# The causal mask of the attention scores: added by TensorE inside the score's bank, where VectorE added it before

## What is computed

```python
s = jnp.einsum('bhmqd,bhmkd->bhmqk', qi, k).astype(jnp.float32) * scale
s = jnp.where(kpos[None, :] <= qpos[:, None], s, -jnp.inf)
p = jax.nn.softmax(s, axis=-1)
...
return jnp.einsum('bhqk,bhkd->bhqd', pd.astype(v.dtype), v)
```

## Time and profile before

| what | before |
|---|---|
| median of three runs | 916.38 us |
| lowest and highest | 915.25 and 921.18 us |
| the profiled execution, its own time | 915.04 us |
| span of its instructions | 913.3 us |
| granted TensorE clock, mean | 0.992 |

### The profile page before, as it was taken

The page is one execution under the profiler, slowest core; times in us unless marked ns, Lnnn a source line. Parts: engine busy times, 40 slices in busy tenths (PEclk is TensorE's granted clock), DMA queues, the critical chain, the costliest instruction groups (busy, mean ns, idle before and its releaser), DMA issues.

```text
span 913.3 us, 16032 instructions
## 1 busy us (share of the span) xinstructions
PE 875.5 (96%) x6422; PEld 820.9 (90%) x6422; DVE 611.5 (67%) x1155; ACT 410.9 (45%) x727; POOL 111.4 (12%) x123
## 2 busy tenths in 40 slices
PE   6999999899999999989999999999999999999996
PEld 6998998898888777888999999999998999999994
DVE  4784687662979789745686478945665776676672
ACT  6456666231011254735344875444344444453451
POOL 0149666100011000400000000100000000000000
PEclk9999999999999899999999999999999999999998
DMA  9454433281452400344665243654453455645741
GB/s 368 169 183 126 123 104 111 79 334 49 140 174 103 184 1 1 93 152 142 215 217 168 94 135 110 220 184 175 149 188 134 141 181 187 229 142 182 231 139 47
DMA packets 37786, 139.41 MB, mean 153 GB/s; under 512 B 4304, under 2 KB 4432, under 8 KB 37456
## 3 DMA queue, kind: packets, MB, share of 16 engines
q1 hardware_dynamic: 37424, 136.90, 43.8%
q10 hardware_dynamic: 288, 1.48, 0.5%
HBM read 137.32 MB, written 1.05 MB: 152 GB/s over the span
## 4 chain that ended last, share of the span: by engine, by line
PE 88%; DVE 7%; issue 2%; ACT 2%; DMA 1%; POOL 0%; DVEq 0%; SPq 0%; ACTq 0%; POOLq 0%
PE psum L578 21%; PE psum L579 21%; PE psum L580 21%; PE psum L577 15%; PE psum L731 3%; PE psum L713 2%; PE psum L652 1%; PE psum L724 1%; DVE h_rows L1748 1%; PE psum L856 1%; DVE w_lo L1594 1%; DVE h_lo L1560 1%; DMA rows<-in_mem 1%; PE psum L641 1%; ACT act_tmp L1219 0%
## 5 line engine op out<-in xcount | busy, mean ns | idle before, releaser
L1594 DVE TENSOR_TENSOR w_lo<-raw,w_hi 128x1024 fp32r<-128x1024 f32 x180 | 212.2, 1222 | 86.2 <-ACT w_hi L1151 85.1
L1151 ACT ACTIVATE w_hi<-raw 128x1024 fp32r<-128x1024 f32 x204 | 206.0, 1052 | 41.3 <-PE psum L580 30.3
L578 PE MATMUL psum<-h_hi,w_hi 128*128 128x256 f32 x704 | 199.5, 283 | 0.6 <-issue 0.6
L579 PE MATMUL psum<-h_lo,w_hi 128*128 128x256 f32 x704 | 199.2, 283 | 0.0
L580 PE MATMUL psum<-h_hi,w_lo 128*128 128x256 f32 x704 | 199.2, 283 | 0.0
L578 PE MATMUL psum<-w_hi,h_hi 128*128 128x256 f32 x576 | 166.6, 289 | 4.1 <-DVE h_lo L1560 4.1
L580 PE MATMUL psum<-w_hi,h_lo 128*128 128x256 f32 x576 | 163.7, 284 | 0.0
L579 PE MATMUL psum<-w_lo,h_hi 128*128 128x256 f32 x576 | 163.6, 284 | 0.0
L578 PEld LDWEIGHTS psum<-h_hi,w_hi 128*128 128x128 f32 x704 | 135.1, 192 | 1.6 <-issue 1.4
L579 PEld LDWEIGHTS psum<-h_lo,w_hi 128*128 128x128 f32 x704 | 135.1, 192 | 0.2
L580 PEld LDWEIGHTS psum<-h_hi,w_lo 128*128 128x128 f32 x704 | 135.1, 192 | 0.0
(11 more groups left out here) (276 smaller groups left out, 1138.5 us busy)
## 6 DMA issues: line engine op xcount, KB each, us to landing
raw<-in_blocks SPq DMA_DIRECT2D x208, 512.0 KB, 4.4
first<-in_blocks SPq DMA_DIRECT2D x40, 512.0 KB, 4.8
w_late<-in_blocks SPq DMA_DIRECT2D x4, 512.0 KB, 7.6
early<-in_early SPq DMA_DIRECT2D x1, 1579.0 KB, 16.3
attention<-in_late ACTq DMA_DIRECT2D x1, 1376.0 KB, 6.9
rows<-in_mem SPq DMA_DIRECT2D x2, 512.0 KB, 4.3
x<-in_x SPq DMA_DIRECT2D x1, 1024.0 KB, 8.4
out_x<-h_rows SPq DMA_DIRECT2D x2, 512.0 KB, 2.6
```

The lines of the kernel that those rows point to most:

```text
L578: nc.tensor.matmul(out, lhs[0], rhs[0], start=start, stop=False, skip_group_check=shared_bank)
L579: nc.tensor.matmul(out, lhs[0], rhs[1], start=False, stop=False, skip_group_check=shared_bank)
L1151: nc.scalar.activation(split_part(w_hi, q), raw[:, q % RAW_SLOTS, :], ACT.Copy).then_inc(w_hi_ready, 1)
L1594: V.tensor_tensor(split_part(w_lo, q), raw[:, q % RAW_SLOTS, :], split_part(w_hi, q).bitcast(F32), ALU.subtract).then_inc(w_lo_vector, 1)
```

## The change

The triangle is added by TensorE. After the score product of a causal unit for a half t, a second product accumulates onto the diagonal block of that half: the identity times the triangle, both as fp32r tiles of 128 x 128. VectorE's addition is dropped. ScalarE makes the two fp32r tiles once, ahead of its copy of the memory keys, and TensorE waits for them once, ahead of the first layer's units.

```diff
+        mask_parts = sb("mask_parts", [P, 2, P], F32R)
...
                         mm = nc.tensor.matmul(psum[:, SCORE_BANK + score.slot(i + j), u.seg(t)],
-                                              q[:, t * P:(t + 1) * P], k[:, 0:u.keys[t]], start=True, stop=True)
+                                              q[:, t * P:(t + 1) * P], k[:, 0:u.keys[t]], start=True, stop=True,
+                                              skip_group_check=u.causal)
+                        if u.causal:
+                            at = u.seg(t).start + t * P
+                            mm = nc.tensor.matmul(psum[:, SCORE_BANK + score.slot(i + j), at:at + P], mask_parts[:, 0, :],
+                                                  mask_parts[:, 1, :], start=False, stop=True, skip_group_check=True)
...
+            pe.wait_ge(mask_ready, 1)
             chunk_read(pe, "b_v")
...
             act.wait_ge(lam_neg_exp, 1)
+            act.wait_ge(loaded["early"], 16)
+            link(nc.scalar.activation(mask_parts[:, 0, :], ident, ACT.Copy))
+            nc.scalar.activation(mask_parts[:, 1, :], E("causal")[:, 0:P], ACT.Copy).then_inc(mask_ready, 1)
+            act.wait_ge(mask_ready, 1)
             source("mk0", mk_t[:, 0], 1.0)
...
                     link(V.tensor_tensor(bank[:, 0:u.width], bank[:, 0:u.width], E("cmp_mask"), ALU.add))
-                elif u.causal:
-                    corners = [v.rearrange("p (b k) -> p b k", k=P)[:, 0:3:2, :] for v in (bank[:, 0:3 * P], E("causal"))]
-                    link(V.tensor_tensor(corners[0], corners[0], corners[1], ALU.add))
```

More of the change, by code:

```diff
@@ L442, in build @@
         ws_ready = sem("ws_ready")
+        mask_ready = sem("mask_ready")
         rest_done = sem("rest_done")
```

## The result

The changed kernel takes 972.36 us (median of four runs, 964.80 to 978.07) against 918.72 us for the kernel before beside it (four runs, 915.25 to 921.18): a ratio of 1.058 [1.050, 1.067]. It is slower, as forecast, by 53.6 us and not by 32, and lies above the range. The four executions of the changed kernel differ among themselves as their clock does: spans of 963.0, 969.0, 972.2 and 976.3 us go with mean granted clocks of 0.972, 0.963, 0.962 and 0.957. Its profiled execution is the shortest of them, 964.80 us with a span of 963.0; against the profiled execution of before that is 49.7 us of span.

What follows compares the result with a forecast made beforehand. TensorE, busy for 96% of the span, was taken as the bound. 915.04 us profiled plus 34.9 for mask products less 2.7 of waits is 947.2, and 1.34 more for the median gives 948.5 us; range 934 to 959.

Steps and rivals of the forecast that it cites:

- The pair: TensorE, last transpose to next load in a causal pair: 3.24 us instead of 1.06, 34.9 us more in 16 pairs.
- the sum: Whole kernel: 915.04 us profiled plus 34.9 less 2.7 is 947.2; as a median 948.5 us.
- changes of height: TensorE in a causal pair: each switch between tile heights leaves about 0.10 us empty; six more cost 1.24 us.
- the units' company: TensorE in a causal pair: the two units' scores no longer share the array, costing 0.65 us.
- The waits in the second layer: TensorE's four waits ahead of the second layer's transposes end: 2.7 us off, least nothing, about 3 at most.
- VectorE's later scores: A pair's scores reach VectorE up to 2 us later, covered by projection products: costed at nothing.
- ScalarE's two copies: Two 128 x 128 copies ahead of the memory keys' copy: 0.8 us, absorbed by ScalarE's idle time.
- The narrow fp32r stream: Rival: mask products stream as slowly as plain fp32, 0.216 us instead of 0.06; 958 us in all; chance 0.13.
- The loads: Rival: six more weight loads in a pair hide behind streams, 10.3 us less, 938 us in all; chance 0.12.
- merely take its place: Rival: mask products only join TensorE's row, 0.11 us each, pairs still side by side; 921 us; chance 0.06.
- VectorE does not bind: Denies the rival that VectorE binds and its relief makes the kernel 2 us faster, 914 us; chance 0.03.
- The clock falls: Rival: more drained, idle unit time lowers TensorE's clock; ten microseconds at 1.2 GHz add 5 us; 954 and more; chance 0.04.

Runs made afterwards that it cites:

- e1_grouped: Changed kernel with all scores of a causal pair first, then its four mask products: 923.10 us, ratio 1.005.
- e4_by_half: Changed kernel with, per half, both units' scores and then both mask products: 928.97 us, ratio 1.011.
- e2_no_mask: Changed kernel with the causal mask left out on both VectorE and TensorE: 914.06 us, ratio 0.997.
- e6_wide: Changed kernel with one mask product of 256 columns for each unit, behind all scores of the pair: 919.76 us, ratio 1.001.
- e5_thin: Kernel before plus ten fp32 products of one column at the head of each causal pair: 978.73 us, ratio 1.065.
- e9_refill_more: Changed kernel plus eighteen fp32r products of 256 columns at the head of each causal pair: 998.92 us, ratio 1.089.
- e8_dense: Kernel before plus five fp32 products of 256 columns at the head of each causal pair: 950.49 us, ratio 1.034.
- e11_spread: Changed kernel plus three products of 256 columns behind each of the first three mask products of a causal pair: 974.53 us, ratio 1.061.

## Why the prediction was right or wrong

**The pair: right.** The forecast was 3.24 us where it was 1.06; 3.21 were measured in the first layer, and over all 16 pairs of the profiled execution the added time, at full clock, is 34.9 us, the sum's own figure. That the two agree so closely is in part luck: from the last mask to the values 0.17 us were measured where the sum has 0.11, and from each of the three others to the next score 0.25 where it has 0.27. Scores no longer start together, as was said. e1_grouped and e4_by_half put the two units side by side again and took six and four changes of height out of a pair, and the time went with them; no run took the units' company away alone, so its 0.65 us is read from the timeline, where each unit's scores stream by themselves.

**The waits in the second layer: nearly right.** 2.7 us were taken off; 1.6 of the 2.0 us of waits in the earlier trace rows went, the second stretch of e2_no_mask is 2.0 us shorter than before, and its whole time bounds the relief at some 3. VectorE's later scores and ScalarE's two copies cost nothing, as said: the rest of the span is unchanged.

**The rivals that fell.** The narrow fp32r stream is not slow: 0.125 us for a whole mask product between its like in e1_grouped, and 0.17 to the values. The loads don't hide at a change of height: the mask's load starts with its product, after 0.33 us idle. The rule of the Trainium skill ("TensorE: Matmul & The Clock Gate", "Part 2: What happens when you issue a matmul"), by which loads are pulled ahead, shows here only where the height stays the same: the values' load, 0.06 us ahead. The mask does not merely take its place, unless it is put behind the scores as in e6_wide; VectorE does not bind, since e2_no_mask gains only 0.35%.

**The step that failed: "The clock falls".** The prediction saw that "more of the units' time is drained and idle", gave that 0.04, and priced it at ten microseconds at the lower level, 5 us; the sum itself has it at nothing. The profiled execution spends some 23 us of the first stretch and (1 - 0.90) x 2 x 98.2 = 20 of the second at half clock, where the second had 5 before. At 0.44 that is 10.3 + 6.6 = 16.9; the span leaves 49.7 - 34.9 + 2.0 = 16.8 (the 0.44 comes from the first stretch, so only the second tests it). The other executions, at 0.957 to 0.963, lose 6 to 13 us more. So the mechanism was named and its size was off by three to six times (16.8 to 30 us, not 5), and its chance was far too small. What misled was the reading of the earlier trace rows: the clock is 1.00 wherever TensorE is busy and falls only after it had stood waiting, and from this I took it that a TensorE which never waits keeps its clock. That reading was wrong, and the trace of the kernel before shows it in narrower windows around the 0.77 (columns as in the earlier trace rows) and in the group of records there:

```profile
304.00:307.70 3.70, 3.70 (x34) 3.65 (x32) 3.39 (x15) 0.60 (x1) 0.00 (x0) 1.00 0.99 402
307.80:308.50 0.70, 0.70 (x5) 0.54 (x4) 0.08 (x1) 0.21 (x1) 0.00 (x0) 0.50 0.02 6
308.50:310.00 1.50, 0.00 (x1) 0.00 (x0) 0.56 (x3) 0.24 (x1) 0.00 (x0) 0.50 0.00 0
...
L577 PE MATMUL psum<-first 128*128 128x24 f32 x32 | 3.8, 271 | 0.0
```

The clock is at half from 307.8 us, while TensorE is busy, and TensorE stands waiting only from 308.5 on. At that moment it was near the end of 32 records of 24 columns in a row. So the kernel before already had a fall behind short products, with TensorE busy until then; e5_thin, which adds one-column products to each pair, shows the same at a clock of 0.87.

The same page of the Trainium skill, "Part 1: The HAM clock gate (the \"warmup\" mystery)", says that the throttled state is the default and that activity lifts it, by how busy TensorE has recently been. The two levels agree with the trace. "Busy" can't be read as the profile's busy time, though: between 170 and 180 us it is 10.00 of 10 us at a clock of 0.66.

## What to carry to other kernels

When an edit puts single short products between products of another tile height, price every change of height (here six more in a pair are 1.24 us of the 2.15, by the prediction's price), and then look at the granted clock in narrow windows, busy TensorE or not: here its fall cost half as much again as the stalls themselves. Group such products behind the whole row of the others, and make one wide product of two narrow ones, as e6_wide does: the same additions then cost 1 us, which can't be told from nothing, instead of 54. And before moving work off an engine, leave it out once: some 3 us was all there was to win.

## What was not expected of the hardware

- A busy share of 100% says nothing of the clock: e5_thin and e8_dense add equal time to the same kernel, both with TensorE busy throughout, and run at 0.87 and 1.00 in the first stretch.
- Dense work ahead of a thin stretch does not protect it (e9_refill_more, 0.89 with eighteen products at the head of each pair); inside it, it mostly does (e11_spread, 0.98 with nine).
- A microsecond at half clock costs 0.44 us here, not 0.5: the projection products, most of TensorE's work, go from 0.12 to 0.21 us and not to twice the time.
- The executions of the kernel after spread over 13 us (964.8 to 978.1), longer where the clock is lower. A low clock alone does not spread them: e5_thin, with the lowest, lies between 977.0 and 980.0.
